# The last down-projection tile, split by tokens: 144 tokens first, the other 144 into banks of their own

## What is computed

```python
def rmsnorm(x, g):
    xf = x.astype(jnp.float32)
    y = xf * lax.rsqrt(jnp.mean(xf * xf, axis=-1, keepdims=True) + EPS)
    return (y * g.astype(jnp.float32)).astype(x.dtype)

def ffn_sublayer(x, norm_ffn_g, w_gate, w_up, w_down):
    xn = rmsnorm(x, norm_ffn_g)
    h = jax.nn.silu(jnp.einsum('bld,df->blf', xn, w_gate)) * jnp.einsum('bld,df->blf', xn, w_up)
    return x + jnp.einsum('blf,fd->bld', h, w_down)
...
y_prompt = rmsnorm(hp, final_norm_g)
y_sample = rmsnorm(hs, final_norm_g)
```

## Time and profile before

| | |
|---|---|
| median of 3 runs | 1177.46 us (1177.36 to 1177.7) |
| the profiled execution's own time | 1176.95 us |
| its span in the trace | 1175.2 us |
| PE busy | 1163.5 us (99%) |
| DVE busy | 763.1 us (65%) |
| ACT busy | 501.6 us (43%) |
| last tile's products | 1160.22 to 1163.58 us |
| first output multiply starts | 1166.34 us |
| last output multiply ends | 1172.28 us |

### The profile page before, as it was taken

One profiled execution on the slowest core, in us unless ns is written; L12 is line 12 of the kernel. 1 busy time (PEld: TensorE's weight loads), 2 busy tenths in 40 slices (PEclk: granted clock), 3 DMA queues, 4 the chain that ended last, 5 costly groups with the idle time before them and its releaser, 6 DMA issues.

```text
span 1175.2 us, 22032 instructions
## 1 busy us (share of the span) xinstructions
PE 1163.5 (99%) x8718; PEld 1162.8 (99%) x8718; DVE 763.1 (65%) x1154; ACT 501.6 (43%) x624; POOL 18.4 (2%) x52
## 2 busy tenths in 40 slices
PE   9999999999999999999999999999999999999996
PEld 9999999999999999999999999999999999999996
DVE  6799999977875644754646456465565465645655
ACT  8544535446643334333343343333333333333345
POOL 0000010000000000000000000000000000000003
PEclk9999999999999999999999999999999999999998
DMA  9665555555555555545555555555555555555542
GB/s 331 209 189 167 160 149 164 171 170 165 158 168 172 163 164 164 167 145 184 161 162 165 169 165 161 161 160 170 167 163 143 181 164 170 164 161 161 163 153 86
DMA packets 105241, 197.08 MB, mean 168 GB/s; under 512 B 7792, under 2 KB 10992, under 8 KB 105200
## 3 DMA queue, kind: packets, MB, share of 16 engines
q1 hardware_dynamic: 102512, 194.34, 54.6%
q10 hardware_dynamic: 2688, 2.18, 0.6%
HBM read 193.00 MB, written 3.49 MB: 167 GB/s over the span
## 4 chain that ended last, share of the span: by engine, by line
PE 98%; DVE 0%; DMA 0%; issue 0%; ACT 0%; DVEq 0%
PE bank L1234 32%; PE bank L1236 32%; PE bank L1235 32%; PE bank L1269 1%; PE bank L1273 1%; PE bank L1277 1%; DMA x_sb<-in_x 0%; DVE x_sb L1181 0%; PE bank L1326 0%; PE bank L1212 0%; PE bank L1220 0%; DVEq L150 0%; DVE s_bc L1173 0%; PE bank L1306 0%; DVE norm L1167 0%
## 5 line engine op out<-in xcount | busy, mean ns | idle before, releaser
L707 DVE TENSOR_TENSOR wl<-raw,wh 128x1024 fp32r<-128x1024 f32 x358 | 436.1, 1224 | 355.7 <-ACT wh L465 355.2
L465 ACT ACTIVATE wh<-raw 128x1024 fp32r<-128x1024 f32 x358 | 378.9, 1060 | 600.7 <-PE bank L1236 597.1
L1234 PE MATMUL bank<-xh_sb,wh 128*128 128x288 f32 x1872 | 554.3, 296 | 0.0
L1235 PE MATMUL bank<-xl_sb,wh 128*128 128x288 f32 x1872 | 552.2, 295 | 0.0
L1236 PE MATMUL bank<-xh_sb,wl 128*128 128x288 f32 x1872 | 550.4, 294 | 0.0
L1236 PEld LDWEIGHTS bank<-xh_sb,wl 128*128 128x128 f32 x1872 | 352.6, 188 | 0.0
L1235 PEld LDWEIGHTS bank<-xl_sb,wh 128*128 128x128 f32 x1872 | 351.4, 188 | 0.0
L1234 PEld LDWEIGHTS bank<-xh_sb,wh 128*128 128x128 f32 x1872 | 350.8, 187 | 0.0
L1234 PE MATMUL bank<-mh_sb,wh 128*128 128x288 f32 x960 | 284.2, 296 | 0.0
L1235 PE MATMUL bank<-ml_sb,wh 128*128 128x288 f32 x960 | 283.2, 295 | 0.0
L1236 PE MATMUL bank<-mh_sb,wl 128*128 128x288 f32 x960 | 282.3, 294 | 0.0
(11 more groups left out here) (177 smaller groups left out, 350.9 us busy)
## 6 DMA issues: line engine op xcount, KB each, us to landing
raw<-in_w_gate SPq DMA_DIRECT2D x88, 512.0 KB, 3.7
raw<-in_w_up SPq DMA_DIRECT2D x88, 512.0 KB, 3.6
raw<-in_w_down SPq DMA_DIRECT2D x88, 512.0 KB, 3.9
raw<-in_w_in SPq DMA_DIRECT2D x62, 512.0 KB, 4.4
raw<-in_w_out SPq DMA_DIRECT2D x32, 512.0 KB, 4.2
x_sb<-in_x SPq DMA_DIRECT2D x7, 288.0 KB, 6.6
out_y<-x_sb SPq DMA_DIRECT2D x7, 288.0 KB, 2.3
raw<-in_w_in ACTq DMA_DIRECT2D x4, 256.0 KB, 5.3
```

What stands on the lines that cost most here:

```text
L465: act.activation(slot(wh, t), slot(raw, t), ACT.Copy).then_inc(hi_ready, 1)
L707: dve.tensor_tensor(slot(wl, t), slot(raw, t), slot(wh, t).bitcast(F32), ALU.subtract).then_inc(lo_ready, 1)
L1234: pe.matmul(banks[n][:, 0:T], W_H[:, k, cols], hi_, start=(first and k == 0), stop=False)
L1235: pe.matmul(banks[n][:, 0:T], W_H[:, k, cols], lo_, start=False, stop=False)
```

## The change

The last tile is no longer multiplied with all 288 tokens. `half_block(n, k, h)` multiplies it with 144. First come all 24 products for tokens 0 to 143 (h = 0), accumulated on the strip's banks as before; then 24 products for tokens 144 to 287 (h = 1), which go to two other banks (`rest_bank(0)` and `rest_bank(1)`, two column blocks in each). The sums for the first half's norm (`last_sums(0)`, `last_statistic(0)`) stand among the first products of the rest. DVE adds the banks in halves: `half_residual(0, n)` for the first half, `half_residual(1, n)` for what the strip's first tile left for the rest, and `rest_residual(i)` for the last tile's share of the rest, two blocks at a time. The squares are added up per half (`half_sum`), and the gains of the last four blocks are made per half (`half_gain`). The pieces of the first half are mixed with this work. The diff:

```diff
@@ -300,6 +300,7 @@
         ffn_silu, ffn_scaled = sem("ffn_silu"), sem("ffn_scaled")
         ffn_sig, h_hi, h_lo = sem("ffn_sig"), sem("h_hi"), sem("h_lo")
         a_stored, b_stored, v_stored, c_stored = (sem(n) for n in ("a_stored", "b_stored", "v_stored", "c_stored"))
+        half_full, half_added, rest_added = sem("half_full"), sem("half_added"), sem("rest_added")
         last_sq, y_ready, y_stored = sem("last_sq"), sem("y_ready"), sem("y_stored")
         y_gained, s3_root, polished = sem("y_gained"), sem("s3_root"), [sem(f"polished{h}") for h in range(2)]
         SEMS = {"b_out": b_out, "vt_ready": vt_ready, "var_used": var_used, "d_cent": d_cent, "a_cent": a_cent, "z_biased": z_biased}
@@ -347,6 +348,9 @@
                 self.n += 1
                 ins.then_inc(self.s, 1)
                 self.eng.wait_ge(self.s, self.n)
+
+        def rest_bank(i):
+            return bank[use_of(S_END + D // GRP, i) % BANKS]
 
         def misc_bank(name):
             return bank[BANKS + MISC_AT[name] % 2]
@@ -683,18 +687,39 @@
                     m = (t - T_END) // PER_DN - 1
                     last_squares(range(m * NG, m * NG + NG))
                     gain(m)
-            last_squares(range(KD - NG, KD - 1))
-            for h in range(2):
-                act.wait_ge(banks_free, use_of(S_END, KD - 1) + 1 + h)
-                act.activation(last_square(KD - 1)[:, TOKENS[h]], X[:, KD - 1, TOKENS[h]], ACT.Square).then_inc(last_sq, 1)
-            for h, name in enumerate(("s3a", "s3b")):
+
+            def half_square(n):
+                act.wait_ge(half_added, n + 1)
+                act.activation(SQ[:, n, TOKENS[0]], X[:, KD - NG + n, TOKENS[0]], ACT.Square).then_inc(last_sq, 1)
+
+            def rest_squares(i):
+                ns = slice(i * TK, i * TK + TK)
+                act.wait_ge(half_added, NG + i + 1)
+                act.activation(SQ[:, ns, TOKENS[1]], X[:, KD - NG + i * TK:KD - NG + i * TK + TK, TOKENS[1]],
+                               ACT.Square).then_inc(last_sq, TK)
+
+            def half_gain(h):
+                for b in range(KD - NG, KD):
+                    act.activation(gained(slice(b, b + 1))[:, 0, TOKENS[h]], X[:, b, TOKENS[h]], ACT.Copy,
+                                   scale=v("final_norm_g", b)).then_inc(y_gained, 1)
+
+            def last_rsqrt(h):
+                name = ("s3a", "s3b")[h]
                 act.wait_ge(misc_full, MISC_AT[name] + 1)
                 act.activation(SETS[0][1][:, TOKENS[h]], misc_bank(name)[:, TOKENS[h]], ACT.Abs_reciprocal_sqrt,
                                bias=eps[:, :]).then_inc(s3_root, 1)
+
+            for n in range(NG):
+                half_square(n)
+            act.wait_ge(sums, 1)
+            last_rsqrt(0)
+            half_gain(0)
+            rest_squares(0)
+            rest_squares(1)
+            last_rsqrt(1)
             act.wait_ge(s3_root, 2)
             act.activation(SETS[0][2][:, TOKENS[1]], SETS[0][1][:, TOKENS[1]], ACT.Square, scale=0.5 ** 0.5).then_inc(polished[1], 1)
-            act.wait_ge(sums, 1)
-            gain(KD // NG - 1)
+            half_gain(1)
 
 
         @block.vector
@@ -1140,21 +1165,32 @@
                     for n in range(NG):
                         residual(s * NG + n, strip_block(S_END + s, n, t))
 
-            s, t = D // GRP - 1, TILES - 1
-            for n in range(NG - 1):
-                residual(s * NG + n, strip_block(S_END + s, n, t))
-                if n == 1:
-                    dve.wait_ge(sums, 1)
-                    dve.wait_ge(last_sq, KD - NG + 1)
-                    dve.tensor_tensor(one_sq, sum_sq, SQ[:, 0, :], ALU.add).then_inc(sums_dve, 1)
-                if n == 2:
-                    dve.wait_ge(last_sq, KD - NG + 2)
-                    dve.wait_ge(sums_dve, 1)
-                    dve.tensor_tensor(one_sq, one_sq, SQ[:, 1, :], ALU.add).then_inc(sums_dve, 1)
-            src = strip_block(S_END + s, NG - 1, t)
-            for h in range(2):
-                dve.tensor_tensor(X[:, KD - 1, TOKENS[h]], src[:, TOKENS[h]], X[:, KD - 1, TOKENS[h]], ALU.add).then_inc(banks_free, 1)
-
+
+            def half_residual(h, n):
+                src, ts = bank[use_of(S_END + D // GRP - 1, n) % BANKS], TOKENS[h]
+                dve.wait_ge(half_full, n + 1)
+                dve.tensor_tensor(X[:, KD - NG + n, ts], src[:, ts], X[:, KD - NG + n, ts], ALU.add).then_inc(rest_added if h else half_added, 1)
+
+            def rest_residual(i):
+                dst = X[:, KD - NG + i * TK:KD - NG + i * TK + TK, TOKENS[1]]
+                dve.wait_ge(rest_added, i * TK + TK)
+                dve.wait_ge(half_full, NG + i + 1)
+                dve.tensor_tensor(dst, blocks(rest_bank(i)[:, 0:T], TK), dst, ALU.add).then_inc(half_added, 1)
+
+            def half_sum(h, i):
+                ts = TOKENS[h]
+                dve.wait_ge(last_sq, KD - NG + h * NG + i + 1)
+                if i:
+                    dve.wait_ge(sums_dve, 2 * h + 1)
+                dve.tensor_tensor(one_sq[:, ts], (one_sq if i else sum_sq)[:, ts], SQ[:, i, ts], ALU.add).then_inc(sums_dve, 1)
+
+            half_residual(0, 0)
+            half_residual(0, 1)
+            dve.wait_ge(sums, 1)
+            half_sum(0, 0)
+            half_residual(0, 2)
+            half_sum(0, 1)
+            half_residual(0, 3)
 
             def halved_square():
                 dve.wait_ge(s3_root, 1)
@@ -1177,20 +1213,27 @@
                 h, bs = PIECES[i]
                 n = bs.stop - bs.start
                 dve.wait_ge(polished[h], 3)
-                dve.wait_ge(y_gained, KD if h else bs.stop)
+                dve.wait_ge(y_gained, KD + NG if h and bs.stop > KD // 2 else KD if h else bs.stop)
                 dve.scalar_tensor_tensor(out=Y[:, h, bs, :], in0=gained(bs)[:, :, TOKENS[h]], scalar=1.0,
                                          in1=s_bc[:, TOKENS[h]].unsqueeze(1).to_broadcast([P, n, HT]),
                                          op0=ALU.mult, op1=ALU.mult).then_inc(y_ready, 1)
 
+            for n in range(NG):
+                half_residual(1, n)
             halved_square()
             times_var(0)
             last_root(0)
             piece(0)
+            rest_residual(0)
             piece(1)
+            half_sum(1, 0)
+            half_sum(1, 1)
+            rest_residual(1)
+            piece(2)
             times_var(1)
-            piece(2)
+            piece(3)
             last_root(1)
-            for i in range(3, len(PIECES)):
+            for i in range(4, len(PIECES)):
                 piece(i)
 
 
@@ -1352,19 +1395,56 @@
                     products(t, strip_banks(S_LOOP + i), lambda k: (xh[:, base + k, :], xl[:, base + k, :]), kt == 0,
                              kt == tiles - 1, g * (NG * S_BODY) + (use_of(S_LOOP + i, 0) - BANKS + 1),
                              (h_lo, g * NG + NG) if j == PER else None)
-            for t in range(T_END, TILES):
+            for t in range(T_END, TILES - 1):
                 s, kt = divmod(t - T_END, PER_DN)
                 tile(t, S_END + s, kt, PER_DN, MH, ML, kt * TK, (h_lo, (NF - 1) * NG + kt * TK + TK) if s == 0 else None)
 
-
-            for h, name in enumerate(("s3a", "s3b")):
-                M, ts = into(name), TOKENS[h]
-                pe.wait_ge(sums_dve, 2)
-                pe.matmul(M[:, ts], ones_d[:, :], one_sq[:, ts], start=True, stop=False)
-                pe.wait_ge(last_sq, KD - 1)
-                pe.matmul(M[:, ts], ones_d[:, :], SQ[:, NG - 2, ts], start=False, stop=False)
-                pe.wait_ge(last_sq, KD + h)
-                pe.matmul(M[:, ts], ones_d[:, :], SQ[:, NG - 1, ts], start=False, stop=True).then_inc(misc_full, 1)
+            t = TILES - 1
+            banks = strip_banks(S_END + D // GRP - 1)
+            W_H, W_L = (slot(x, t).rearrange("p (k n) -> p k n", k=TK) for x in (wh, wl))
+
+            def half_block(n, k, h):
+
+                cols, m, ts = slice(n * P, (n + 1) * P), NG - TK + k, TOKENS[h]
+                out = rest_bank(n // TK)[:, n % TK * HT:n % TK * HT + HT] if h else banks[n][:, ts]
+                pe.matmul(out, W_H[:, k, cols], MH[:, m, ts], start=h == 1 and k == 0, stop=False)
+                pe.matmul(out, W_H[:, k, cols], ML[:, m, ts], start=False, stop=False)
+                mm = pe.matmul(out, W_L[:, k, cols], MH[:, m, ts], start=False, stop=k == TK - 1)
+                if k == TK - 1 and (h == 0 or n % TK == TK - 1):
+                    mm.then_inc(half_full, 1)
+
+            S3 = [misc_bank(name) for name in ("s3a", "s3b")]
+
+            def last_sums(h):
+
+                ts = TOKENS[h]
+                pe.wait_ge(sums_dve, 2 * h + 2)
+                pe.matmul(S3[h][:, ts], ones_d[:, :], one_sq[:, ts], start=True, stop=False)
+                pe.wait_ge(last_sq, KD - NG + h * NG + NG - 1)
+                pe.matmul(S3[h][:, ts], ones_d[:, :], SQ[:, NG - 2, ts], start=False, stop=False)
+
+            def last_statistic(h):
+
```

(20 more changed lines are left out.)

## The result

The changed kernel takes 1180.21 us (median of 11 runs, 1179.91 to 1180.84) against 1177.35 us for the kernel before in the same sessions (11 runs): 2.86 us more, a ratio of 1.0026 with a 95% interval of 1.0018 to 1.0034. It is slower. The forecast was 1180.1.

A forecast was written before the change was run, and what follows sets the result against it. PE's products fill all but the two ends, so only the tail's dependent chain and DVE's output pieces count: 3.00 us more after piece 0 less 0.43 before it, +2.6 on the median 1177.46, gives 1180.1; range 1178.8 to 1181.5.

The forecast's parts named there:

- item 1: PE, last tile: a 144-column product costs 0.11 us, held up by a weight load that is not halved.
- A: Rival: the narrow product costs as much as the wide one, 0.133 us; +3.3, with low clock +3.8; chance 0.25.
- B: Rival: the narrow product costs half, 0.067 to 0.08 us; +1.5 to +1.8, down to +1.1; chance 0.12.
- C: Rival: the narrow product falls to plain float32 speed, 0.245 us; +7.0 us; chance 0.10.
- item 2: First half up to output piece 0: piece 0 starts 0.43 us earlier; the four extra DVE adds cost nothing.
- item 4: Piece 0 to the end, after the change: 8.94 us, 3.00 more than before, with DVE idle about 1.7.
- item 5: Output transfers: hiding half the traffic gains little; tail behind the last piece unchanged at 2.9 us, at best 0.4 less.
- the second limit: Output tail: DMA engines full at 384 GB/s, 0.77 us of transfer per full piece against 0.67 on DVE.
- The clock: PE during the last sums: full 2.4 GHz taken (0.37); at 1.2 GHz four passes cost 0.49 more, +3.1 (0.13).
- The sum: Whole kernel: 3.00 - 0.43 = 2.57, say +2.6 us, giving 1180.1 against the median.
- no difference: Outcome that the time stays the same, within about 0.2% (2.36 us) of the kernel before; chance 0.24.

The follow-up runs named there:

- wide-products kernel: Changed kernel's order on DVE and ACT, but the last tile multiplied with all 288 columns as before: ratio 1.0029, +3.59 us against the kernel before.
- rest-first kernel: Changed kernel with both adds of the rest right behind the first output piece, pieces 2 and 3 before the second half's variance step: ratio 1.0021, +2.13 us against before.
- half-output kernel: Kernel before, without sending the first half's output; DVE still makes all pieces: ratio 1.0000 against before.
- narrow products alone: Kernel before with each last-tile product made as two of 144 columns, old order and banks: ratio 1.0017, +2.03 us against before.
- the order alone: Changed DVE and ACT order with 288-column products, plus 28 idle-time products keeping PE busy: +3.57 us by medians against before, 3.2 by trace stages.
- three-parts kernel: Kernel before with three products of 96 columns for each of 288 in the last tile: +6.9 us against before (one run).

## Why the prediction was right, point by point

*The narrow product (item 1).* Taken 0.11 from the transposes, measured 0.112, and 2.52 us from the first to the 24th where I had 2.53. Rivals A (0.133), B (half price) and C (plain float32 speed) are all out. This was the choice on which most of the range hung, and the nearest row, though of another type and 128 columns, gave it.

*To piece 0 (item 2).* Expected 0.43 sooner, measured 0.34. The last sum of the first half starts at 1164.58, 3.79 after the first product, exactly the 3.79 of the working; the 0.09 lie between it and the root, which starts 0.55 later instead of 0.45. DVE's four extra adds did cost nothing: they end at 1164.79, and DVE then waits 0.76 for the root.

*From piece 0 on (item 4).* Expected 8.94, measured 9.00; `times_var(1)` expected 4.87 after piece 0, measured 4.95; the idle time ahead of it expected about 1.7, measured 1.49, since piece 2 ended at 3.46 instead of 3.18: it follows `rest_residual(1)` by 0.37, where I had 0.22, and I had counted its step of 0.67, not its length of 0.75. The wide-products kernel shows that the new order makes this stretch long with the old products too (9.12 with the clock up), and the rest-first kernel that the place of the add is 0.8 us of it.

*The transfers (item 5).* Taken as unchanged, measured 2.83 against 2.92. The 0.4 that I allowed at best were not there to be had, as the half-output kernel shows, and the second limit that I saw in the full DMA engines bound nothing. Item 5 also says that four pieces are out before DVE stops; by item 4, and in the trace, it is three (piece 3 starts at 1171.74, behind the wait).

*The clock.* In the changed kernel's trace it stays at 1.00 until the last sums are through, the case that I took, but only just. The last four passes start between 1169.95 and 1170.5, the root at 1170.75, and the windows have the fall here (clock third from the end):

```profile
1170.50:1171.00 0.50, 0.21 (x2) 0.00 (x0) 0.00 (x0) 0.25 (x1) 0.00 (x0) 0.78 0.23 88
```

A mean of 0.78 puts it at about 1170.8 (an estimate). That it came after the sums in the profiled execution was luck: in seven of the eleven runs the mean granted clock is 0.996 instead of the profiled one's 0.997, and their median is 1180.45 us against 1180.07 for the other four. So the low clock probably has a part in the medians' +2.86, which is 0.23 more than the two traces give. Where it fell early, the price was near the one that I had set: 0.66 for six passes in rest-first, 0.58 for four in the wide products, where I wrote 0.49 for four.

*The sum.* +2.6 forecast, +2.63 by the stages of the two traces, +2.86 by the medians. That the stages agree to 0.1 is in part luck: 0.09 too little gained ahead of piece 0 and 0.06 too much behind it stand against 0.09 less in the tail. The chance of 0.24 for "no difference" was fair: the interval's lower end, 1.0018, lies inside 0.2%.

*What the two parts cost together* is less than their sum: narrow products alone +2.15 in the trace, the order alone +3.2, both +2.63. In the changed kernel the doubled products lie beside the first half's norm, which was the aim; the order on DVE then gives away what that hid.

## What to carry to other kernels

A product with a fresh 128 x 128 weight load cost 0.11 us here at every width from 48 to 144 columns: splitting the moving side of 288 columns in two costs 1.7 times the PE time, so look for the nearest row with few columns before splitting. When a dependent chain (add, square, sum, root) is to run beside other work, put its first step at the head of the in-order queue as soon as its input exists; here an add whose input had been there for 1.9 us stood behind an output piece that nobody waited for, and DVE's next step for that norm came 2.6 us after it. Moving it gave back 0.8 us, not the 3: before, the second half's norm had been ready in time, and the split put adds, sums and waits between the pieces that were not there. Full DMA engines in a tail are no proof that the transfers set its end: halve the traffic and look.

## What the hardware did that I had not expected

The clock fell while PE was working without a gap. In the three-parts kernel, from the last tile's first product at 1160.28 on, PE made products of 96 columns back to back; at about 1166.2 the granted clock went from 1.00 to 0.50 and the steps from 0.11 to 0.21 us. Windows (busy time and instructions of PE first, the clock third from the end), then the timeline:

```profile
1165.50:1166.00 0.50, 0.50 (x7) 0.50 (x6) 0.00 (x0) 0.00 (x0) 0.00 (x0) 1.00 0.00 0
1166.00:1166.50 0.50, 0.50 (x6) 0.50 (x5) 0.00 (x0) 0.00 (x0) 0.00 (x0) 0.71 0.00 0
1166.50:1167.00 0.50, 0.50 (x4) 0.50 (x4) 0.50 (x2) 0.01 (x1) 0.00 (x0) 0.50 0.00 0
```

```profile
1166.02 0.27 PE L1237 MATMUL bank<-ml_sb,wh 128*128 128x96 f32 x1
...
1166.48 0.41 PE L1237 MATMUL bank<-ml_sb,wh 128*128 128x96 f32 x1
```

That is 5.9 us after the first of them, and the reason why its first piece came 7.0 us later instead of 4.8. The clock was back (0.96 from 1173.0 to 1173.5, 1.00 behind it) when PE, busy all the while at the lower level, came to the end of the last sums. With 144 columns, and with 240 and 48 in turn, the clock stayed up through the 48 products, but these last only 5.4 us, so they don't tell whether the width made the difference; the changed kernel kept PE busy for 6.0 us with 144 columns and the first half's sums, and stayed at 1.00. The Trainium skill (page "TensorE: Matmul & The Clock Gate", section "The HAM clock gate (the "warmup" mystery)") has the clock follow how busy TensorE has recently been; that agrees with the fall in the idle stretches above, but by the profile's count PE was 100% busy here. One trace shows it, and its cause stays open; whether a longer run of narrow products costs more than 0.11 us each in other executions, too, I have not tried.
